# Sums of squares added on VectorE ahead of the product with ones, in a chain of two transformer-like blocks

## The reference

```python
def rmsnorm(x, w):                       # over the 1024 features of each token
    return x * rsqrt(mean(x * x, -1) + 1e-6) * w

for i in range(2):                       # first block: two layers
    h = rmsnorm(x, norm_mix[i])
    x = x + (gla_mixer(h) if i == 0 else attn_mixer(h))     # each ends in "@ w_out"
    x = x + conv_ffn(rmsnorm(x, norm_ffn[i]))               # up (5632 columns), conv of 3, silu gate, down
# second block: one layer
h = rmsnorm(x, norm_g) * (1 + scale) + shift                # scale, shift, gate from c
p = h @ w_in                                                # 9344 columns, then conv and rwkv branches
x = x + gate * (m @ w_out)
return rmsnorm(x, final_g)
```

## Time and profile before

| | us |
|---|---|
| three runs, median (lowest to highest) | 1054.8 (1054.6 to 1055.06) |
| the profiled execution, its own time | 1054.78 |
| its span in the profile | 1053.0 |
| PE busy, share of the span | 98% |
| DVE busy | 83% |
| ACT busy | 58% |

### The profile page before, as it was taken

One profiled execution on the slowest core, in us unless ns is written; L12 is line 12 of the kernel. 1 busy time (PEld: TensorE's weight loads), 2 busy tenths in 40 slices (PEclk: granted clock), 3 DMA queues, 4 the chain that ended last, 5 costly groups with the idle time before them and its releaser, 6 DMA issues.

```text
span 1053.0 us, 23926 instructions
## 1 busy us (share of the span) xinstructions
PE 1027.3 (98%) x10150; PEld 950.8 (90%) x10150; DVE 873.6 (83%) x1455; ACT 611.9 (58%) x878; POOL 18.3 (2%) x38
## 2 busy tenths in 40 slices
PE   7999999999999999999999999999999999999997
PEld 6999999999999989999998998889999988889997
DVE  7865689999889886998898897988998999965473
ACT  7744664444446666644434477556667667676443
POOL 2000000000000000000000000000000000000000
PEclk9999999999999999999999999999999999999999
DMA  9652266776654515477675746323323322234431
GB/s 281 211 183 94 81 220 220 240 243 218 217 164 161 175 60 180 163 240 237 228 233 184 212 129 192 121 85 119 122 87 117 122 82 82 82 122 161 161 121 41
DMA packets 135927, 168.20 MB, mean 160 GB/s; under 512 B 3200, under 2 KB 125056, under 8 KB 135584
## 3 DMA queue, kind: packets, MB, share of 16 engines
q1 hardware_dynamic: 131936, 153.44, 45.3%
q0 software_dynamic: 3904, 13.50, 3.9%
HBM read 164.83 MB, written 2.10 MB: 159 GB/s over the span
## 4 chain that ended last, share of the span: by engine, by line
PE 76%; DVE 16%; ACT 5%; DMA 1%; issue 1%; POOL 0%; DVEq 0%; SPq 0%; ACTq 0%; POOLq 0%
PE banks L350 13%; PE banks L315 10%; PE banks L316 8%; PE banks L317 8%; PE banks L352 6%; DVE w_parts L277 3%; DVE hf L2543 3%; PE banks L652 2%; PE bank L654 2%; PE bank L652 2%; DVE w_parts L301 2%; PE bank L656 2%; PE banks L654 2%; PE banks L656 2%; ACT w_parts L272 1%
## 5 line engine op out<-in xcount | busy, mean ns | idle before, releaser
L277 DVE TENSOR_TENSOR w_parts<-raw,w_parts 128x2048 fp32r<-128x2048 f32 x95 | 217.0, 2288 | 28.1 <-ACT w_parts L272 27.7
L350 PE MATMUL banks<-x_parts,w_parts 128*128 128x512 f32 x640 | 227.1, 399 | 0.0
L315 PE MATMUL banks<-x_parts,w_parts 128*128 128x256 f32 x704 | 211.5, 300 | 0.0
L316 PE MATMUL banks<-x_parts,w_parts 128*128 128x256 f32 x736 | 207.8, 282 | 0.0
L317 PE MATMUL banks<-x_parts,w_parts 128*128 128x256 f32 x704 | 198.7, 282 | 0.0
L272 ACT ACTIVATE w_parts<-raw 128x2048 fp32r<-128x2048 f32 x95 | 180.9, 1905 | 3.6 <-PE banks L820 2.1
L352 PE MATMUL banks<-x_parts,w_parts 128*128 128x256 f32 x640 | 179.8, 281 | 0.0
L350 PEld LDWEIGHTS banks<-x_parts,w_parts 128*128 128x128 f32 x640 | 120.4, 188 | 29.0
L315 PEld LDWEIGHTS banks<-x_parts,w_parts 128*128 128x128 f32 x704 | 134.0, 190 | 9.9 <-issue 3.6
L316 PEld LDWEIGHTS banks<-x_parts,w_parts 128*128 128x128 f32 x736 | 140.6, 191 | 0.6 <-issue 0.5
L317 PEld LDWEIGHTS banks<-x_parts,w_parts 128*128 128x128 f32 x704 | 134.3, 191 | 0.0
(11 more groups left out here) (413 smaller groups left out, 2411.5 us busy)
## 6 DMA issues: line engine op xcount, KB each, us to landing
raw<-in_ffn_w_up SPq DMA_DIRECT2D x44, 1024.0 KB, 5.1
raw<-in_w_in SPq DMA_DIRECT2D x36, 1024.0 KB, 5.4
raw<-in_ffn_w_down SPq DMA_DIRECT2D x22, 1024.0 KB, 5.3
big<-in_ada_w_t POOLq DMA_DIRECT2D x24, 512.0 KB, 4.1
raw<-in_gla_w_in SPq DMA_DIRECT2D x11, 1024.0 KB, 5.6
raw<-in_attn_w_qkv SPq DMA_DIRECT2D x6, 1024.0 KB, 5.0
raw<-in_gla_w_out SPq DMA_DIRECT2D x4, 1024.0 KB, 5.0
raw<-in_attn_w_out SPq DMA_DIRECT2D x4, 1024.0 KB, 5.0
```

The lines of the kernel that those rows point to most:

```text
L277: eng.tensor_tensor(WL[:, n % RING, :, :], RAW[:, n % RING, :, :], WH[:, n % RING, :, :].bitcast(F32), ALU.subtract).then_inc(w_lo_ready, 1)
L315: nc.tensor.matmul(ps, wh, xh, start=start, stop=False)
L316: nc.tensor.matmul(ps, wh, xl, start=False, stop=False)
L350: nc.tensor.matmul(PS[bank + m].rearrange("p (a t) -> p a t", a=2), WH[:, s, k, ms], XP[:, :, k, :], start=k == 0, stop=False, skip_group_ ...
```

## The change

`added_sums` is new on PE. Norms 1 and 3 (i odd): DVE adds the squares of tiles 0 to 5 into tile 0 with three instructions that stand in `add_projection` at j == 3, in front of the wait for the last block of the projection; PE multiplies three tiles (0, 6, 7) with ones instead of eight, in front of the last k of `early_product`. Norms 2 and 4 (i even): DVE adds tiles 4 to 7 to tiles 0 to 3 with one instruction of 128x1024 in `mlp`, behind the last `early_low` and in front of two `split_lo`; PE multiplies four tiles with ones after the whole product. `early_product` now goes k by k over both halves. The first early block of norm 4 goes through `early_product` too.

```diff
--- before.py
+++ after.py
@@ -597,25 +597,38 @@
                         last = nc.tensor.matmul(PS[3][:, 0:T], ones, HF[:, k, :], start=k == 0, stop=k == KT - 1)
                 last.then_inc(sem("square_sums"), 1)
 
-            def early_product(i, n, bank):
+            def added_sums(i):
+
+                pe.wait_ge(sem("squares_added"), i)
+                tiles_left = (0, 6, 7) if i % 2 else (0, 1, 2, 3)
+                if i % 2:
+                    pe.wait_ge(sem("squares_ready"), 4 * i + 4)
+                for k in tiles_left:
+                    last = nc.tensor.matmul(PS[3][:, 0:T], ones, HF[:, k, :], start=k == 0, stop=k == tiles_left[-1])
+                last.then_inc(sem("square_sums"), 1)
+
+            def early_product(i, n, outs):
 
                 eh, el = EARLY[i]
                 pe.wait_ge(w_lo_ready, n + 1)
                 s = n % RING
-                for m in range(2):
-                    for k in range(KT):
-                        if m == 0 and k % 2 == 0:
-                            pe.wait_ge(sem("early_split"), 4 * i + k // 2 + 1)
-                        last = three(PS[bank][:, m * T:(m + 1) * T], WH[:, s, k, m * P:(m + 1) * P],
-                                     WL[:, s, k, m * P:(m + 1) * P], eh[:, k, :], el[:, k, :], k == 0, k == KT - 1)
-                        if m == 0 and k % 2:
-                            pe.wait_ge(sem("squares_ready"), 4 * i + k // 2 + 1)
-                            for kk in (k - 1, k):
-                                summed = nc.tensor.matmul(PS[3][:, 0:T], ones, HF[:, kk, :], start=kk == 0,
-                                                          stop=kk == KT - 1)
-                            if k == KT - 1:
-                                summed.then_inc(sem("square_sums"), 1)
+                one_bank = len(outs) == 1
+                for k in range(KT):
+                    if k % 2 == 0:
+                        pe.wait_ge(sem("early_split"), 4 * i + k // 2 + 1)
+                    for m in range(2):
+                        ps = PS[outs[0]][:, m * T:(m + 1) * T] if one_bank else PS[outs[m]][:, 0:T + 2]
+                        ms = slice(m * P, (m + 1) * P)
+                        nc.tensor.matmul(ps, WH[:, s, k, ms], eh[:, k, :], start=k == 0 and (m == 0 or not one_bank),
+                                         stop=False, skip_group_check=True)
+                        nc.tensor.matmul(ps, WH[:, s, k, ms], el[:, k, :], start=False, stop=False, skip_group_check=True)
+                        last = nc.tensor.matmul(ps, WL[:, s, k, ms], eh[:, k, :], start=False, stop=k == KT - 1,
+                                                skip_group_check=True)
+                    if i % 2 and k == KT - 2:
+                        added_sums(i)
                 last.then_inc(block_done, 1)
+                if i % 2 == 0:
+                    added_sums(i)
 
             def out_projection(n0, a0, xh, xl, ready=None):
 
@@ -660,7 +673,7 @@
                     ins.then_inc(block_done, 1)
 
                 pe.wait_ge(out_added, 6 if layer else 3)
-                early_product(2 * layer + 1, n0, 2)
+                early_product(2 * layer + 1, n0, (2,))
                 pe.wait_ge(sem("rstd_ready"), 2 * layer + 2)
                 product(pe, n0 + 1, 3, *EARLY[2 * layer + 1])
                 up(n0 + 2, 1, ready=ready)
@@ -944,7 +957,7 @@
                 if m:
                     last.then_inc(block_done, 1)
 
-            early_product(2, N_QKV, bank_of(N_QKV))
+            early_product(2, N_QKV, (bank_of(N_QKV),))
             pe.wait_ge(sem("rstd_ready"), 3)
             for tt in range(2):
                 last = nc.tensor.transpose(PS[3][:, T + tt * P:T + (tt + 1) * P], RS[:, tt * P:(tt + 1) * P], ident)
@@ -1006,24 +1019,15 @@
 
             mlp(1, N_F1, E_F1)
 
-            def early_last(j, banks, summed):
+            def early_last(j, banks):
 
                 n, (eh, el) = N_L3 + j, EARLY[4]
                 pe.wait_ge(w_lo_ready, n + 1)
                 for m in range(2):
                     ms = slice(m * P, (m + 1) * P)
                     for k in range(KT):
-                        if summed and m == 0 and k % 2 == 0:
-                            pe.wait_ge(sem("early_split"), 16 + k // 2 + 1)
                         last = three(PS[banks[m]][:, 0:T + 2], WH[:, n % RING, k, ms], WL[:, n % RING, k, ms],
                                      eh[:, k, :], el[:, k, :], k == 0, k == KT - 1)
-                        if summed and m == 0 and k % 2:
-                            pe.wait_ge(sem("squares_ready"), 16 + k // 2 + 1)
-                            for kk in (k - 1, k):
-                                sums_done = nc.tensor.matmul(PS[3][:, 0:T], ones, HF[:, kk, :], start=kk == 0,
-                                                             stop=kk == KT - 1)
-                            if k == KT - 1:
-                                sums_done.then_inc(sem("square_sums"), 1)
                 last.then_inc(block_done, 1)
 
             def lora():
@@ -1272,8 +1276,8 @@
                         last.then_inc(sem("rwkv_out_summed"), 1)
 
             pe.wait_ge(evacuated, E_L3)
-            early_last(0, (2, 1), True)
-            early_last(1, (4, 5), False)
+            early_product(4, N_L3, (2, 1))
+            early_last(1, (4, 5))
             for u in range(8):
                 if u < 4:
                     pe.wait_ge(sem("rms_split"), 16 + u + 1)
@@ -2004,6 +2008,11 @@
                         lo_by_halves(n0 + j + 2)
                     elif lo_from <= j < 3:
                         lo(n0 + j + 2)
+                    if j == 3:
+                        for g in (1, 2):
+                            dve.wait_ge(sem("squares_ready"), 4 * early[0] + g + 1)
+                            ch.step(v.tensor_tensor(HF[:, 0:2, :], HF[:, 0:2, :], HF[:, 2 * g:2 * g + 2, :], ALU.add))
+                        v.tensor_tensor(HF[:, 0, :], HF[:, 0, :], HF[:, 1, :], ALU.add).then_inc(sem("squares_added"), 1)
                     dve.wait_ge(block_done, n0 + j + 1)
                     ps = PS[bank_of(n0 + j)][:, :].rearrange("p (m t) -> p m t", m=2)
                     d = dst[:, 2 * j:2 * j + 2, :]
@@ -2019,7 +2028,7 @@
                 dve.wait_ge(block_done, n0 + 1)
                 times_rstd(U[:, 0, :, 1:T + 1], 2)
 
-            def mlp(layer, n0, e0, early=None):
+            def mlp(layer, n0, e0, early):
                 g0, g1 = layer * FI, layer * (FI + 1)
                 cw, cb = COL["ffn_w_conv"] + 132 * layer, COL["ffn_b_conv"] + 44 * layer
 
@@ -2139,10 +2148,11 @@
                     x = X[:, 2 * q:2 * q + 2, :]
                     v.tensor_tensor(x, x, PS[4 + q][:, :].rearrange("p (m t) -> p m t", m=2), ALU.add)\
                         .then_inc(sem("x_ready"), 1)
-                    if early and q:
+                    if q:
                         early_low(early[0], q - 1, early[1])
-                if early:
-                    early_low(early[0], 3, early[1])
+                early_low(early[0], 3, early[1])
+                dve.wait_ge(sem("squares_ready"), 4 * early[0] + 4)
+                v.tensor_tensor(HF[:, 0:4, :], HF[:, 0:4, :], HF[:, 4:8, :], ALU.add).then_inc(sem("squares_added"), 1)
                 split_lo(dve, n0 + 3 * FI + 1)
 
             v.memset(w_up, 0.0).then_inc(sem("zeroed"), 1)
```

## The result

The changed kernel takes 1058.49 us (median of 7 runs, 1058.03 to 1058.78), the kernel before 1055.04 (7 runs beside them, 1054.47 to 1055.17). The ratio is 1.0033 with a 95% interval of [1.0024, 1.0042]: slower by 3.45 us, where 3.4 was forecast. The span went from 1053.0 to 1056.6.

What follows compares the result with a forecast made beforehand. The prediction took DVE's sequence to start the next stage at norms 1, 3 and 4, and PE to pace only norm 2. 0 + 0.45 + 1.80 + 1.15 = 3.4 us on 1054.8 gave 1058.2; 8-in-10 range 1055.8 to 1059.8.

Steps and rivals of the forecast that it cites:

- Norm 1: 0: Behind the GLA mixer: three DVE additions, needing 1.8 us, fall into DVE's 3.21 us wait at L2010; no time change.
- The wait in front of the down product: At norm 1, PE's wait for DVE's L2070, forecast at over 1 us.
- Norm 2: +0.45: Behind the first feed-forward: the 128x1024 addition delays ACT's squares by 1.15, so PE starts `qk_sums(0)` 0.45 us later.
- The slack of 0.77: At norm 2, ACT's squares for `qk_sums(0)` were ready 0.77 us before PE needed them; forecast as used up.
- Norm 3: +1.80: Behind the attention: three DVE additions before L2010, covered by no wait, move L2070 and the down product by 1.8 us.
- The price of 0.73 for a dependent addition: At norm 3, each of two dependent 128x512 DVE additions takes 0.73 us from start to start.
- Norm 4: +1.15: Behind the second feed-forward: the 128x1024 DVE addition delays the last normed tile, SP's store, the load and L1126 by 1.15 us.
- the rival by which the load would take the delay up: Likeliest at norm 4: the load behind the store swallows a big delay; 1055.2 to 1057.0 us, at 1056.2; chance 0.20.
- PE's 7.7 us: Over all four norms PE saves 18 matmuls with ones at 0.43 us each, forecast to be spent in waits.
- The rival that PE decides: Whole kernel: PE's 98% is real backlog, the additions fit beside it, 7.7 us go; 1047.1 us; chance 0.08.
- the root is ready before DVE is: At norms 2 and 4, the root comes before DVE can start the norm: 340.2 against 340.97 at norm 2.

## Why the prediction was right

The time was forecast at 1058.2 and came at 1058.49. As the trace has them, the four steps are 0.02, 0.50, 1.79 and 1.13 us. Together they are 3.44, beside 3.45 between the medians, and none is off by more than 0.05, so the forecast did not hit by errors that cancel. By its steps:

- *Norm 1: 0.* Measured 0.02 at the norm and 0 in a run of its own. The wait in front of the down product was forecast at over 1 us and is 1.48.
- *Norm 2: +0.45.* 0.43 at `qk_sums(0)`; by L2019 at j = 2 of norm 3 (417.15 against 416.41) the shift without the scatter is 0.52. The slack of 0.77 was used up as worked out. This is the one step for which the norm alone was neither taken back nor run as changed; that the squares are the cause is shown by the run that moves them, in which the wait is gone and `qk_sums(0)` starts 0.45 earlier than before, where the prediction had put it (at 346.3; 346.37).
- *Norm 3: +1.80.* 1.79 on DVE; with the additions alone 1.78 on DVE and 1.81 in the time; 1.7 in the time and 1.81 in the trace when they are taken out. The price of 0.73 for a dependent addition held: the two records are 1.41 long together and the third starts at 1.45. The Trainium skill reports of a row of copies on DVE that a semaphore after each cost nothing extra (VectorE: DVE Perf Modes, section The DRAIN you can't avoid). Taken as a rule for these additions, with the 0.61 of this trace, it would have given 1.56; the run of the additions alone has 1.78.
- *Norm 4: +1.15.* 1.13 on the chain, 1.15 when it is taken back. The delay passed through SP's store and the load whole: the load landed 7.89 us after its issue against 7.88, so the rival by which the load would take the delay up did not happen.
- *PE's 7.7 us: worth nothing.* They were worth nothing alone either: that run's ratio is 1.0007, of which the new order explains 0.5 us, and by its interval it gains 0.2 us at most. The rival that PE decides is refuted by that run, and with it the reading of 98% busy as the bound; the Trainium skill's rule to begin with the engine of highest occupancy (Perfetto Trace Analysis, section Identifying the Most-Contended Engine) would have led there. It judges TensorE by its weight loads and not by its matmuls, but those were busy for 90% here, still more than DVE's 83%.

The sum has no term for the new order on PE, and rightly: the prediction says that the root is ready before DVE is, and in the changed kernel DVE's norm waits for it neither at norm 2 nor at norm 4. Without the additions the same order costs about 0.5 us at norm 4, as was expected before that run.

## What to carry to other kernels

A busy share near 100% does not make an engine the bound at the place of an edit: follow the chain through that place, and ask whether the engine that gets the work has a gap there or is already the one the next stage waits for. Of the additions in four places, those at norm 1 were free because the engine stood waiting for 3.21 us, and those at norms 3 and 4 were paid in full because no wait stood behind them to take them up. Saved work on an engine that then waits turns into the wait, and at norm 2 a short slack on another engine (0.77 us) decided how much was paid.

## What the runs showed of the hardware

Two dependent DVE additions of 128x512 start 0.73 us apart. Where the next instruction doesn't need the result, it starts 0.60 after one of this size: L2070 of the earlier trace rows at 164.66 behind the row below. So the wait for one's own result costs some 0.12 to 0.13.

```profile
164.06 0.68 DVE L2077 TENSOR_TENSOR u<-u,banks 128x512 f32<-128x512 f32 x1
```

A load of 1 MB, issued right behind the store of `X`, took 7.88 us from SP's issue to landing before, and 7.89 after, with the issue 3.65 later. That is 2.5 more than the median of such loads; that the store is the reason is likely and not shown. The granted clock of PE over the span was 0.999 of full speed before and 0.998 in the changed kernel, in spite of its waits of 1.4 us; single executions of the kernel before show 0.998, too.
